# Latent product: slots of an adaptive chunk used alternately with those of a latent chunk, and two q or k products in one PSUM bank

## The chip, the cores and the metric

The kernel runs on one core of one Trainium2 chip. The metric is the device time of one execution in microseconds, and the median of the runs is what is compared. The engines are TensorE (PE; its weight loads are PEld), VectorE (DVE), ScalarE (ACT), GpSimd (POOL) and SyncE (SP), which issues most loads. One profiled execution gives the trace; its times are microseconds from the start of its span.

## What is computed

Two blocks act on 256 tokens of width 2048. The first (attention, a recurrent group, a layer of 16384 experts of which rows are gathered) isn't touched by the change. The second has two layers, each with adaptive parameters: a shift, a scale and a gate computed from a conditioning vector. Cut to what matters here:

```python
def ada_params(cond, w, b):
    mod = jax.nn.silu(cond) @ w + b          # 2048 -> 6144, for each layer
    return jnp.split(mod, 3, axis=-1)

xm_l = x_lat * (1.0 + sc_l) + sh_l
proj = xm_l @ w_in                           # 256 x 2048 @ 2048 x 7184
q, k, v, o, z_m, gates, u_p, z_p = split(proj)
qk = silu(dwconv_centered(concatenate([q, k], -1), conv_qk))   # three taps along the tokens
```

The product `xm_l @ w_in` for the latent tokens is the stage in question; the mLSTM scan and a pooling branch use its parts.

## The kernel before

**Plan.** Everything that TensorE multiplies by comes through a ring of four slots in SBUF, 128 x 2048 fp32 (1024 KB) each. The class `Plan` (lines 89 to 160) numbers in advance each load, each PSUM unit (a unit takes bank number unit modulo 8) and each "piece". `make_plan` writes the order out by hand, and the engines' programs follow the same order. SP goes through `plan.loads` in order (line 488 issues): load n waits for the release of load n-4, which was in the same place of the ring, and nothing behind it is issued before that.

**Adaptive chunks.** The 24 chunks of 512 columns of the adaptive weights take four slots each. `ada_chunk(c)` multiplies each slot with the conditioning vectors in four column groups of 32 (line 645); a slot is released as soon as TensorE has used it. Then `ada_rows` on ACT copies the result, `ada_turn(c)` on TensorE turns it (line 656), and `ada_columns` on ACT adds the bias (line 1041). Chunk 15 and chunks 16 to 21 are spread over the latent stage: `LAT_ADA` says ahead of which latent chunk each one is computed.

**Latent chunks.** `LAT` is the order: l_q 0 and 1, l_k 0 and 1, l_g, l_v 0 and 1, l_u 0 and 1, l_o 0 and 1, l_zp 0 and 1, l_z 0 and 1. A chunk is 512 columns of the weights with all 2048 rows, in four slots; each slot is two pieces. The fp32 product is made of three products of halves: ACT copies a piece to its hi half (`split_hi`, line 1016), DVE (q, k, v; line 1494) or POOL (u, o, zp, z; line 543) subtracts to get the lo half, and TensorE does `split_chunk` (line 623): for each of 16 row tiles, three matmuls for each output. The buffer of pieces holds four. A latent slot is released by the lo half of its second piece.

For q and k the outputs are features by tokens, four of 128 x 256, each in a PSUM unit of its own; for the others two of 128 x 512. DVE's `conv_unit` (lines 1802 to 1804) reads the q and k units in the next chunk's time, among the lo halves. Behind l_u 0 TensorE needs the gate rows, which come from a chain on ACT and DVE (lines 1878 to 1904, 1329); behind l_u 1, l_o 0, l_o 1 and l_zp 0 follow the mLSTM heads (lines 834, 841, 856), and behind l_zp 1 the pooling products (lines 903, 915). After l_z 0 TensorE transposes y, which DVE has to have ready (until line 2025).

ACT's part is `latent_hi`: hi halves 0 to 3, then `ada_columns`, the evacuation of the chunk before, `ada_rows`, then hi halves 4 to 7.

Of the kernel before, what the change touches and what calls it, by code (L numbers as in the profile page):

```python
# [64 lines left out]
def row_slot(n):  # L65
# [14 lines left out]
       ("l_o", 0), ("l_o", 1), ("l_zp", 0), ("l_zp", 1), ("l_z", 0), ("l_z", 1))  # L80
LAT_ADA = {("l_q", 0): 15, ("l_k", 0): 16, ("l_v", 0): 17, ("l_u", 0): 18, ("l_o", 0): 19, ("l_zp", 0): 20,
           ("l_z", 0): 21}
LAT_HEAD = {("l_u", 1): 0, ("l_o", 0): 1, ("l_o", 1): 2, ("l_zp", 0): 3}
# [21 lines left out]
class Plan:  # L105
# [26 lines left out]

    def split_chunk(self, name, c, units):

        for i in range(units):
            self.unit[name, c * units + i] = len(self.unit)
        eng = "pool" if name in LO_POOL else "dve"
        for j in range(8):
            self.piece[name, c, j] = len(self.piece)
            self.lo[eng] += 1  # L140
            self.piece_lo.append((eng, self.lo[eng]))
            if j % 2:
                self.slot[name, c, j // 2] = len(self.loads)
                self.loads.append((name, c, j // 2, 2048))
                self.release.append(("lo_" + eng, self.lo[eng]))
            if j < 7:
                self.piece_used += 1
                self.piece_release.append(("piece", self.piece_used))
            else:
                self.piece_release.append(("unit", self.unit[name, (c + 1) * units - 1]))  # L150
# [27 lines left out]
def make_plan():  # L178
# [31 lines left out]
    p.units("x2T", 8)  # L210
    for step in LAT:
        name, c = step
        if step in LAT_ADA:
            p.gemm(("ada", LAT_ADA[step]), 1, 4, 1, 2048)
        if name == "l_g":
            p.gemm("l_g", 1, 1, 1, 256)
        else:
            p.split_chunk(name, c, 4 if name in ("l_q", "l_k") else 2)
        if step in LAT_ADA:
            p.turn(LAT_ADA[step])  # L220
        if step == ("l_u", 0):
# [28 lines left out]
def build(nc, t, out):  # L250
    plan = make_plan()
    ctx = ExitStack()
    with ctx:
# [297 lines left out]
        def _(pe):  # L551
# [47 lines left out]

            def split_chunk(name, c, hi, lo, features, later=None):  # L600

                n_units = 4 if features else 2
                o = [open_unit((name, n_units * c + i)) for i in range(n_units)]
                for j in range(8):
# [6 lines left out]
                    for kk in range(2):  # L611
                        k = 2 * j + kk
                        whi, wlo = pc[:, 512 * kk:512 * kk + 512], pc[:, 1024 + 512 * kk:1536 + 512 * kk]
                        for i in range(n_units):
# [19 lines left out]

            def ada_chunk(c):


                name = ("ada", c)
                if c == 0:
                    pe.wait_ge(sem("cond_ready"), 1)  # L640
                o = open_unit((name, 0))
                for s in range(4):
                    sl = slot_of(name, 0, s)
                    for j in range(4):
                        m = nc.tensor.matmul(o[32 * j:32 * j + 32, :], cond_s[:, 2 * (4 * s + j):2 * (4 * s + j) + 32],  # L645
                                             sl[:, j * 512:(j + 1) * 512], start=(s == 0), stop=(s == 3))
                    if s < 3:
                        m.then_inc(sem("slot_used"), 1)
                close(m, (name, 0))

# [304 lines left out]
        def _(act):  # L955
# [337 lines left out]
            def latent_hi(name, c, evac=None):  # L1293

                at = LAT.index((name, c))
                before = LAT_ADA.get(LAT[at - 1]) if at else None
                if name == "l_g":
# [4 lines left out]
                else:  # L1302
                    split_hi(name, c, 0, 4)
                if before is not None:
                    ada_columns(before)
                if evac is not None:
                    evac(LAT[at - 1][1])
                if (name, c) in LAT_ADA:
                    ada_rows(LAT_ADA[name, c])
                if name != "l_g":  # L1310
# [115 lines left out]
        def _(dve):  # L1426
# [370 lines left out]

            def conv_unit(name, i, dst, c0):

                wait_unit(dve, (name, i))  # L1800
                x_, y = bank((name, i))[:, 0:S], dst[:, i, :]
# [3 lines left out]
                give(m, (name, i))  # L1805
                gave(dve, (name, i))
                dve.sem_inc(sem("conv_ready"), 1)

# [38 lines left out]
            def lo_and_conv(name, c, units):  # L1847
# [9 lines left out]
            split_lo("l_q", 0)  # L1857
            lo_and_conv("l_q", 1, [("l_q", i, QL2, 0) for i in range(4)])
            lo_and_conv("l_k", 0, [("l_q", i, QL2, 0) for i in range(4, 8)])
            lo_and_conv("l_k", 1, [("l_k", i, KL2, 8) for i in range(4)])  # L1860
# [4 lines left out]
            lo_and_conv("l_v", 0, [("l_k", i, KL2, 8) for i in range(4, 8)])  # L1865
            split_lo("l_v", 1)
# [349 lines left out]
```

## Time and profile before

| | us |
|---|---|
| median of 3 runs (lowest, highest) | 3024.66 (3022.16, 3025.05) |
| the profiled execution | 3025.71 |
| its span | 3023.9 |
| TensorE busy | 1648.0 (54%) |
| DVE busy | 1992.5 (66%) |
| POOL busy | 1244.4 (41%) |
| mean granted TensorE clock | 0.764 |

The page cuts the span into 40 slices of 75.6 us and gives the busy share of each in tenths. The timeline shows instructions in order of time, with the idle time before each and who ended it in brackets. The view of waits sums those idle times by waiter and releaser. The chain of waits goes back from the end to what released each step. The windows give busy time, number of instructions, granted clock (1.00 is 2.4 GHz), DMA share and GB/s of a stretch.

### The profile page before, as it was taken

To read this page: it belongs to the slowest core of one execution; us is meant where nothing else is said; L and a number is where in the kernel's file an instruction comes from. 1 tells how busy PE (TensorE), PEld (TensorE's weight loads), DVE (VectorE), ACT (ScalarE), POOL (GpSimd) and SP (SyncE) were. 2 spreads that over 40 slices of the span, in tenths; PEclk is the share of its full clock that TensorE was granted. 3 is DMA by queue.
4 is the path that set the end of the run, shared out by engine and by line. 5 is a ranking of instruction groups with operands and counts; after the bars stand their busy time and mean duration, and the time that the engine had idled before them with its cause. 6 is when DMAs were issued, how large, how long until landed. Compare 5 with 4: busy or idle time off the path is not lost.

```text
span 3023.9 us, 20189 instructions
## 1 busy us (share of the span) xinstructions
PE 1648.0 (54%) x7536; PEld 1219.8 (40%) x7536; DVE 1992.5 (66%) x2358; ACT 524.0 (17%) x783; POOL 1244.4 (41%) x598
## 2 busy tenths in 40 slices
PE   7994888794700440000000000048999889899987
PEld 3773443681600120000000000038777678588876
DVE  1364120388999979999999999975343536644556
ACT  1014200110100000000000000023333334345432
POOL 0000000033488768888888888820054550000000
PEclk9997789895855775555555555569999999899998
DMA  5442845399999999999999999965544555655543
GB/s 219 141 159 93 333 185 198 138 393 422 421 422 422 417 421 422 421 422 422 422 422 422 422 422 422 422 272 183 196 180 167 183 182 194 256 195 195 195 141 110
DMA packets 122753, 882.31 MB, mean 292 GB/s; under 512 B 13728, under 2 KB 14240, under 8 KB 16416
## 3 DMA queue, kind: packets, MB, share of 16 engines
q0 software_dynamic: 73728, 536.90, 42.7%
q1 hardware_dynamic: 45920, 326.91, 29.5%
q10 hardware_dynamic: 3008, 17.21, 1.5%
q8 instruction: 59, 0.97, 0.1%
q14 instruction: 38, 0.31, 0.0%
HBM read 878.88 MB, written 2.10 MB: 291 GB/s over the span
## 4 chain that ended last, share of the span: by engine, by line
PE 44%; POOL 30%; DMA 10%; DVE 8%; issue 5%; ACT 2%; DVEq 0%; SPq 0%; ACTq 0%
PE psum L623 24%; POOL W L519 18%; POOL early_rows L519 12%; PE psum L593 7%; PE psum L576 6%; DMA early_rows<-in_peer_u,W 3%; DMA ring<-in_ada 3%; DMA W<-in_peer_u,W 3%; PE psum L645 2%; PE psum L856 1%; DVE W L1789 1%; DMA W<-in_peer_v,W 1%; PE psum L696 1%; PE psum L841 1%; PE psum L656 1%
## 5 line engine op out<-in xcount | busy, mean ns | idle before, releaser
L519 POOL DMA_INDIRECT W<-in_peer_u,W x150 | 297.3, 1982 | 746.4 <-DVEq L1771 611.3
L623 PE MATMUL psum<-split,hi 128*128 128x512 f32 x1664 | 524.8, 397 | 46.5 <-POOL split L543 31.5
L696 PE MATMUL psum<-cst,X 128*128 128x128 f32 x64 | 10.4, 340 | 909.8 <-DVEq L1842 909.8
L1494 DVE TENSOR_TENSOR split<-ring,split 128x1024 fp32r<-128x1024 f32 x208 | 252.5, 1225 | 287.3 <-ACT split L1016 285.2
L696 PEld LDWEIGHTS psum<-cst,X 128*128 128x128 f32 x64 | 10.1, 183 | 910.7 <-DVEq L1842 910.7
L1838 DVE SCALAR_TENSOR_TENSOR X<-W,X 128x2048 f32<-128x2048 f32 x154 | 362.1, 2351 | 22.7 <-DMA W<-in_peer_v,W 4.1
L1016 ACT ACTIVATE split<-ring 128x1024 fp32r<-128x1024 f32 x272 | 284.1, 1057 | 490.4 <-PE psum L623 377.7
L1789 DVE CUSTOM_DVE_ANT_0 W<-W,XN 128x2048 f32<-128x2048 f32 x150 | 340.7, 2290 | 42.9 <-DMA W<-in_peer_u,W 42.1
L623 PEld LDWEIGHTS psum<-split,hi 128*128 128x128 f32 x1664 | 318.9, 192 | 118.9 <-issue 52.1
L519 POOL DMA_INDIRECT W<-in_peer_v,W x154 | 338.2, 2196 | 47.5 <-issue 47.5
L543 POOL TENSOR_TENSOR split<-ring,split 128x1024 fp32r<-128x1024 f32 x64 | 157.0, 2478 | 313.8 <-ACT split L1016 313.7
L593 PE MATMUL psum<-HT,ring 128*128 128x256 f32 x1280 | 279.5, 381 | 10.2 <-ACT HT L1196 9.0
L593 PEld LDWEIGHTS psum<-HT,ring 128*128 128x128 f32 x1280 | 244.2, 191 | 44.4 <-ACT HT L1196 9.1
L1789 DVE CUSTOM_DVE_ANT_0 early_rows<-early_rows,XN 128x2048 f32<-128x2048 f32 x106 | 241.5, 2291 | 24.2 <-DMA early_rows<-in_peer_u,W 23.0
L1838 DVE SCALAR_TENSOR_TENSOR X<-early_rows,W,X 128x2048 f32<-128x2048 f32 x102 | 239.8, 2351 | 14.8 <-DMA early_rows<-in_peer_v,W 2.1
L519 POOL DMA_INDIRECT early_rows<-in_peer_u,W x106 | 206.3, 1946 | 91.7 <-DVE W L1789 61.5
L519 POOL DMA_INDIRECT early_rows<-in_peer_v,W x102 | 222.9, 2186 | 31.7 <-issue 31.7
L623 PE MATMUL psum<-split,lo_odd 128*128 128x512 f32 x512 | 200.4, 391 | 0.0
L530 POOL TENSOR_TENSOR lo_odd<-W,hi 128x512 fp32r<-128x512 f32 x8 | 11.5, 1436 | 400.3 <-ACT hi L998 400.2
L645 PE MATMUL psum<-ring,cond_s 128*32 128x512 f32 x768 | 120.1, 748 | 84.0 <-DMA ring<-in_ada 84.0
L576 PE MATMUL psum<-ring,W 128*128 128x512 f32 x336 | 148.2, 604 | 10.3 <-DVEq L1692 7.5
L623 PE MATMUL psum<-split,lo_even 128*128 128x512 f32 x320 | 128.4, 401 | 0.0
(303 smaller groups left out, 2200.1 us busy)
## 6 DMA issues: line engine op xcount, KB each, us to landing
ring<-in_ada SPq DMA_DIRECT2D x96, 1024.0 KB, 7.5
ring<-in_odd SPq DMA_DIRECT2D x48, 1024.0 KB, 4.9
ring<-in_w_out SPq DMA_DIRECT2D x16, 1024.0 KB, 4.9
ring<-in_pq SPq DMA_DIRECT2D x16, 1024.0 KB, 7.6
ring<-in_c_k SPq DMA_DIRECT2D x16, 1024.0 KB, 8.1
ring<-in_c_v SPq DMA_DIRECT2D x16, 1024.0 KB, 7.9
ring<-in_w_even SPq DMA_DIRECT2D x16, 1024.0 KB, 4.8
ring<-in_w_odd SPq DMA_DIRECT2D x16, 1024.0 KB, 4.8
```

The lines of the kernel that those rows point to most:

```text
L519: nc.gpsimd.indirect_dma_start(row, None, t["peer_" + table], bass.IndirectOffsetOnAxis(ap=EIDX[:, c:c + 1], axis=0),).then_inc(full, 16)
L543: nc.gpsimd.tensor_tensor(split[:, to + 1024:to + 2048], ring[:, at:at + 1024], split[:, to:to + 1024], ALU.subtract).then_inc(sem("lo_poo ...
L576: m = nc.tensor.matmul(o[tt][:, 0:width], lhs[:, k, tt * P:(tt + 1) * P], sl[:, kk * width:(kk + 1) * width], start=(k == 0), stop=(k == s ...
L593: m = nc.tensor.matmul(o[m4][:, 0:S], sl[:, kk * 512 + m4 * P:kk * 512 + m4 * P + P], rhs[:, k, :], start=(k == 0), stop=(k == KD - 1))
L623: m = nc.tensor.matmul(dst, lhs, rhs, start=(k == 0 and b == 0), stop=(k == KD - 1 and b == 2))
L645: m = nc.tensor.matmul(o[32 * j:32 * j + 32, :], cond_s[:, 2 * (4 * s + j):2 * (4 * s + j) + 32], sl[:, j * 512:(j + 1) * 512], start=(s = ...
L656: m = nc.tensor.matmul(o[:, 2 * a:2 * a + 2], ADAROW[:, a * P:(a + 1) * P], const("sum4"), start=True, stop=True)
L696: m = nc.tensor.transpose(o[:, kk * S + tt * P:kk * S + (tt + 1) * P], src(2 * i + kk, tt), IDENT)
L1016: A(split[:, 2048 * (n % PIECES):2048 * (n % PIECES) + 1024], ring[:, at:at + 1024], ACT.Copy)\
L1494: TT_(split[:, to + 1024:to + 2048], ring[:, at:at + 1024], split[:, to:to + 1024], ALU.subtract)\
L1789: V.tensor_tensor_reduce(out=row, in0=row, in1=xn3[:, tt, :], scale=1.0, scalar=0.0, op0=ALU.mult, op1=ALU.add, accum_out=PACT[:, c:c + 1])\
L1838: STT(x3[:, tt, :], row, PACT[:, c:c + 1], x3[:, tt, :], ALU.mult, ALU.add)\
```

## The change

Chunk 15 (`LAT_FIRST`) is computed ahead of l_q 0 as before. Each of chunks 16 to 21 is now computed within a latent chunk: 16 in l_q 0, 17 in l_k 0, 18 in l_v 0, 19 in l_u 0, 20 in l_o 0, 21 in l_zp 0. Its four slots are loaded alternately with the latent slots (latent, adaptive, latent, ...), and TensorE uses one after every second piece. An adaptive slot is still released by TensorE. The turn of a chunk comes after the next latent chunk (`LAT_ADAS`). The four q or k outputs of a chunk go to two PSUM units, two halves of 256 columns in each; only the first matmul into a bank carries the start flag, and the unit is closed by its second half. DVE reads both halves and gives the bank back once.

```diff
-LAT_ADA = {("l_q", 0): 15, ("l_k", 0): 16, ("l_v", 0): 17, ("l_u", 0): 18, ("l_o", 0): 19, ("l_zp", 0): 20,
-           ("l_z", 0): 21}
+LAT_FIRST = 15
+LAT_ADA = {("l_q", 0): 16, ("l_k", 0): 17, ("l_v", 0): 18, ("l_u", 0): 19, ("l_o", 0): 20, ("l_zp", 0): 21}
+LAT_ADAS = (LAT_FIRST,) + tuple(LAT_ADA.get(step) for step in LAT)
...
+    def ada_slot(self, c, s):
+
+        name = ("ada", c)
+        if s == 0:
+            self.unit[name, 0] = len(self.unit)
+        self.slot[name, 0, s] = len(self.loads)
+        self.loads.append((name, 0, s, 2048))
+        if s < 3:
+            self.used += 1
+            self.release.append(("used", self.used))
+        else:
+            self.release.append(("unit", self.unit[name, 0]))
+
+    def split_chunk(self, name, c, units, ada=None):
...
                 self.release.append(("lo_" + eng, self.lo[eng]))
+                if ada is not None:
+                    self.ada_slot(ada, j // 2)
...
-    for step in LAT:
+    p.gemm(("ada", LAT_FIRST), 1, 4, 1, 2048)
+    for at, step in enumerate(LAT):
         name, c = step
-        if step in LAT_ADA:
-            p.gemm(("ada", LAT_ADA[step]), 1, 4, 1, 2048)
...
-            p.split_chunk(name, c, 4 if name in ("l_q", "l_k") else 2)
-        if step in LAT_ADA:
-            p.turn(LAT_ADA[step])
+            p.split_chunk(name, c, 2, LAT_ADA.get(step))
+        if LAT_ADAS[at] is not None:
+            p.turn(LAT_ADAS[at])
...
-                                dst = o[i][:, 0:S]
+                                dst = o[i // 2][:, S * (i % 2):S * (i % 2) + S]
...
-                                m = nc.tensor.matmul(dst, lhs, rhs, start=(k == 0 and b == 0),
-                                                     stop=(k == KD - 1 and b == 2))
-                            if k == KD - 1:
-                                close(m, (name, n_units * c + i))
+                                m = nc.tensor.matmul(dst, lhs, rhs,
+                                                     start=(k == 0 and b == 0 and not (features and i % 2)),
+                                                     stop=(k == KD - 1 and b == 2 and not (features and i % 2 == 0)))
+                            if k == KD - 1 and not (features and i % 2 == 0):
+                                close(m, (name, 2 * c + (i // 2 if features else i)))
                     if j < 7:
                         m.then_inc(sem("piece_used"), 1)
+                    if ada is not None and j % 2:
+                        ada_slot(ada, j // 2)
...
+            def ada_slot(c, s):
+
+                name = ("ada", c)
+                if c == 0 and s == 0:
+                    pe.wait_ge(sem("cond_ready"), 1)
+                o = open_unit((name, 0)) if s == 0 else bank((name, 0))
+                sl = slot_of(name, 0, s)
+                for j in range(4):
+                    m = nc.tensor.matmul(o[32 * j:32 * j + 32, :], cond_s[:, 2 * (4 * s + j):2 * (4 * s + j) + 32],
+                                         sl[:, j * 512:(j + 1) * 512], start=(s == 0), stop=(s == 3))
+                if s < 3:
+                    m.then_inc(sem("slot_used"), 1)
+                else:
+                    close(m, (name, 0))
...
-            ada_chunk(LAT_ADA[LAT[0]])
+            ada_chunk(LAT_FIRST)
             wait_split("x2T")
 
             def latent_chunk(name, c):
 
-                ada = LAT_ADA.get((name, c))
-                if ada is not None and (name, c) != LAT[0]:
-                    ada_chunk(ada)
                 if name == "l_g":
                     split_gates("l_g", LO_EVEN)
                 else:
-                    split_chunk(name, c, HI, LO_EVEN, name in ("l_q", "l_k"))
-                if ada is not None:
-                    ada_turn(ada)
+                    split_chunk(name, c, HI, LO_EVEN, name in ("l_q", "l_k"), ada=LAT_ADA.get((name, c)))
+                before = LAT_ADAS[LAT.index((name, c))]
+                if before is not None:
+                    ada_turn(before)
...
+            def conv_unit(name, i, dst, c0, per=1):
+
+                key, half = (name, i // per), i % per
+                if half == 0:
+                    wait_unit(dve, key)
+                x_, y = bank(key)[:, S * half:S * half + S], dst[:, i, :]
...
+                if half == per - 1:
+                    give(m, key)
+                    gave(dve, key)
+                    dve.sem_inc(sem("conv_ready"), per)
+                else:
+                    seq(m)
```

## Rows read from the trace of the kernel before

**Rows 1.** The page, slices: busy tenths of TensorE in 40 slices.
```profile
PE   7994888794700440000000000048999889899987
```

**Rows 2.** Waits of TensorE, 2040 to 2470 us: total, times, longest.
```profile
PE psum L623 <- POOL split L543: 31.5, 5, 7.3
PE psum L623 <- DVE W L1804: 9.7, 3, 8.8
PE psum L623 <- DVE split L1494: 3.8, 2, 3.4
PE psum L645 <- DMA ring<-in_ada: 2.1, 1, 2.1
...
PE psum L880 <- ACT W L1329: 0.5, 1, 0.5
```

**Rows 3.** Timeline: first matmul of l_zp 1; one lo half on DVE.
```profile
2399.48 0.77 PE L623 MATMUL psum<-split,hi 128*128 128x512 f32 x1 [7.30 <-POOL split L543]
...
2042.78 1.23 DVE L1494 TENSOR_TENSOR split<-ring,split 128x1024 fp32r<-128x1024 f32 x1 [1.72 <-ACT split L1016]
```

**Rows 4.** The chain ahead of l_o 0: start us, us, what.
```profile
2273.69 1.04 PE psum L645 x8
...
2274.75 4.94 DMA ring<-in_l_o
...
2279.71 1.06 ACT split L1016
...
2280.84 2.36 POOL split L543
```

**Rows 5.** Windows: busy (instructions) of PE, PEld, DVE, ACT, POOL, granted clock, DMA share, GB/s.
```profile
2151.60:2158.00 6.40, 6.36 (x16) 5.04 (x17) 5.85 (x9) 3.29 (x4) 0.00 (x0) 0.54 1.01 426
2158.00:2177.00 19.00, 19.00 (x90) 15.84 (x88) 8.78 (x12) 13.69 (x15) 0.00 (x0) 1.00 0.51 172
...
2199.60:2203.10 3.50, 3.50 (x33) 0.88 (x32) 0.00 (x0) 0.00 (x0) 0.00 (x0) 1.00 0.37 103
```

**Rows 6.** Windows of line 623: l_q 1, l_k 0, three undisturbed chunks, five late ones.
```profile
2045.00:2070.00 25.00, 23.27 (x192) 23.10 (x192) 1.00 0.38 129
2081.00:2107.50 26.50, 25.23 (x192) 25.06 (x192) 0.91 0.48 172
...
sum 66.30, PE 65.78 PEld 53.55; mean PE 21.93 PEld 17.85
...
sum 122.00, PE 119.49 PEld 96.74; mean PE 23.90 PEld 19.35
```

**Rows 7.** Timeline: four loads issued together, and TensorE using the first and second.
```profile
2594.46 2.90 SPq L488 DMA_DIRECT2D ring<-in_ada  x4
...
2599.34 1.07 PE L645 MATMUL psum<-ring,cond_s 128*32 128x512 f32 x8 [2.37 <-DMA ring<-in_ada]
2601.72 1.94 PE L645 MATMUL psum<-ring,cond_s 128*32 128x512 f32 x8 [1.32 <-DMA ring<-in_ada]
```

**Rows 8.** The chain that ends with the gate rows on TensorE.
```profile
2209.05 1.04 ACT split L1016
...
2214.92 2.72 DVE W L1888
...
2228.66 0.69 DVE W L1899
...
2233.90 0.41 PE psum L880 x4
```

**Rows 9.** Timeline: single rows of POOL, ACT, TensorE and DVE.
```profile
2206.78 21.31 POOL L543 TENSOR_TENSOR split<-ring,split 128x1024 fp32r<-128x1024 f32 x8 [192.54 <-ACT split L1016]
...
2237.54 0.67 ACT L1041 ACTIVATE ada<-psum,col 128x2 f32<-128x2 f32 x4
...
2434.71 3.64 PE L645 MATMUL psum<-ring,cond_s 128*32 128x512 f32 x32
...
2438.73 0.69 DVE L2025 TENSOR_TENSOR XN<-XN,W 128x512 f32<-128x512 f32 x1
```

More of the change, by code:

```diff
@@ L130, in gemm @@
                     self.release.append(("unit", self.unit[name, (c + 1) * units - 1]))
-    def split_chunk(self, name, c, units):
+    def ada_slot(self, c, s):
[10 more added lines that the diff above has]
+    def split_chunk(self, name, c, units, ada=None):
         for i in range(units):
@@ L598, in feature_gemm, with split_chunk @@
                             m.then_inc(sem("slot_used"), 1)
-            def split_chunk(name, c, hi, lo, features, later=None):
-                n_units = 4 if features else 2
-                o = [open_unit((name, n_units * c + i)) for i in range(n_units)]
+            def split_chunk(name, c, hi, lo, features, later=None, ada=None):
+                o = [open_unit((name, 2 * c + i)) for i in range(2)]
                 for j in range(8):
@@ L613, in split_chunk @@
                         whi, wlo = pc[:, 512 * kk:512 * kk + 512], pc[:, 1024 + 512 * kk:1536 + 512 * kk]
-                        for i in range(n_units):
+                        for i in range(4 if features else 2):
                             a = slice(i * P, i * P + P)
@@ L633, in split_gemm @@
                     split_chunk(name, c, HI, lo, False)
+            def ada_slot(c, s):
[11 more added lines that the diff above has]
+                    close(m, (name, 0))
             def ada_chunk(c):
[L638 to L641, printed above, removed]
                 for s in range(4):
[L643 to L649, printed above, removed]
+                    ada_slot(c, s)
             def ada_turn(c):
@@ L1295, in latent_hi @@
                 at = LAT.index((name, c))
-                before = LAT_ADA.get(LAT[at - 1]) if at else None
+                turned = LAT_ADAS[at - 1] if at else None
                 if name == "l_g":
@@ L1303, in latent_hi @@
                     split_hi(name, c, 0, 4)
-                if before is not None:
-                    ada_columns(before)
+                if turned is not None:
+                    ada_columns(turned)
                 if evac is not None:
                     evac(LAT[at - 1][1])
-                if (name, c) in LAT_ADA:
-                    ada_rows(LAT_ADA[name, c])
+                if LAT_ADAS[at] is not None:
+                    ada_rows(LAT_ADAS[at])
                 if name != "l_g":
@@ L1796, in dots_done @@
                 dve.sem_inc(sem("dots_ready"), 1)
-            def conv_unit(name, i, dst, c0):
-                wait_unit(dve, (name, i))
-                x_, y = bank((name, i))[:, 0:S], dst[:, i, :]
+            def conv_unit(name, i, dst, c0, per=1):
[3 more added lines that the diff above has]
+                x_, y = bank(key)[:, S * half:S * half + S], dst[:, i, :]
                 seq(TS(y, x_, column("conv_qk", 16 + c0 + i), None, ALU.mult))
@@ L1804, in conv_unit @@
                 m = STT(y[:, 0:S - 1], x_[:, 1:S], column("conv_qk", 32 + c0 + i), y[:, 0:S - 1], ALU.mult, ALU.add)
-                give(m, (name, i))
-                gave(dve, (name, i))
-                dve.sem_inc(sem("conv_ready"), 1)
+                if half == per - 1:
[4 more added lines that the diff above has]
+                    seq(m)
             topk(0, 0)
@@ L1857, in _ @@
             split_lo("l_q", 0)
-            lo_and_conv("l_q", 1, [("l_q", i, QL2, 0) for i in range(4)])
-            lo_and_conv("l_k", 0, [("l_q", i, QL2, 0) for i in range(4, 8)])
-            lo_and_conv("l_k", 1, [("l_k", i, KL2, 8) for i in range(4)])
+            lo_and_conv("l_q", 1, [("l_q", i, QL2, 0, 2) for i in range(4)])
+            lo_and_conv("l_k", 0, [("l_q", i, QL2, 0, 2) for i in range(4, 8)])
+            lo_and_conv("l_k", 1, [("l_k", i, KL2, 8, 2) for i in range(4)])
             slot = plan.slot["l_g", 0, 0]
@@ L1864, in _ @@
                 GATE_W[:, 0:256], ALU.subtract).then_inc(sem("gate_w_lo"), 1)
-            lo_and_conv("l_v", 0, [("l_k", i, KL2, 8) for i in range(4, 8)])
+            lo_and_conv("l_v", 0, [("l_k", i, KL2, 8, 2) for i in range(4, 8)])
             split_lo("l_v", 1)
```

## The prediction

> **What bounds the kernel now.** I read the page's slices first, to find what each stage waits for [rows 1]. From slice 8 to slice 26 TensorE has next to nothing to do: that is the stage of gathered rows, which the diff doesn't touch. The latent products begin at 2018.7 us, in slice 27, and from there TensorE is busy at eight to nine tenths. What is left to win there is its idle time, and the time it spends at the lower clock. The view of waits of TensorE over the latent stage (2040 to 2470 us) has nearly all of its idle time [rows 2]: 31.5 us in five waits on POOL's lo halves, 9.7 in three on a convolution of DVE (one of them 8.8), 3.8 in two on DVE's lo halves (one of them 3.4), 2.1 for an adaptive slot, and 0.5 for the gate rows. Of the five on POOL the longest, 7.30 us, stands ahead of l_zp 1, which has no adaptive chunk ahead of it [rows 3]. The other four (31.5 - 7.3 = 24.2) stand ahead of l_u 0, l_o 0, l_zp 0 and l_z 0; the 8.8 ahead of l_k 0, the 3.4 ahead of l_v 0, and the 2.1 inside the adaptive chunk ahead of l_v 0. All of these belong to an adaptive chunk: 24.2 + 8.8 + 3.4 + 2.1 = 38.5 us.
>
> The releaser named (a lo half) is the last link only. The chain [rows 4] has the whole of it for l_o 0: TensorE uses an adaptive slot (1.04), only then can SP load a latent slot into that place of the ring of four (4.94), then come ACT's hi half (1.06) and POOL's lo half (2.36). All four places held the adaptive chunk, so nothing of the latent chunk was there early.
>
> Each pause costs a second time. Right behind one the granted clock is 0.54, which is the 1.2 GHz level for nearly the whole stretch, and from 2158 us it is 1.00 [rows 5]. By the windows of line 623 [rows 6] an undisturbed chunk takes 23.27 us (l_q 1) or 21.93 (mean of l_v 1, l_u 1, l_o 1). Behind a pause l_k 0 takes 25.23, and l_v 0, l_u 0, l_o 0, l_zp 0 and l_z 0 take 119.49 together, where 5 x 21.93 is 109.65. That is 1.96 + 9.84 = 11.8 us.
>
> **The change part by part.** The adaptive products 16 to 21 move from ahead of their latent chunk into the latent chunk before, one slot after every two pieces. LAT_FIRST (15) stays. 24 slots are used in a new place; the number of matmuls, loads and turns is the same.
>
> *The pauses.* Loads now alternate, latent and adaptive. Load n waits for the release of load n-4, so the first two latent slots of a chunk wait for lo halves of pieces 1 and 5 of the plain chunk before it, both long before that chunk ends. The tight one is the fourth. SP issues in order, so it goes one issue behind the third adaptive load, which waits until TensorE has used adaptive slot 0; call that moment e. Four loads issued together at 2594.46 landed at 2599.34 and 2601.72, 4.88 and 7.26 us later [rows 7]. So the latent slot is there at e + 7.26. With 1.06 of ACT, 2.36 of POOL [rows 4] and 0.2 for handing on, piece 6 is ready at e + 10.9; with DVE's 1.23 [rows 3], e + 9.8. TensorE reaches piece 6 after four pieces (4 x 21.93/8 = 10.97) and two adaptive slots (2 x 1.04): e + 13.05. The slack is 2.1 us on POOL's chunks and over 3 on DVE's. The third latent slot waits for an early lo half and has more; an adaptive slot issued at e is wanted a whole period after it lands. l_v 0 stands behind the one slot of l_g: its second adaptive load is asked for when l_g ends and its third latent load right behind, wanted 13.05 us later, so the slack is the same. I put all 38.5 us at gone, and with them the 11.8 of low clock.
>
> *Two products in one bank.* l_q 1 and l_k 1 wait for a convolution (9.7 - 8.8 = 0.9 us [rows 2]) that must empty the bank they open. Half as many banks are opened, and the one taken then was emptied a chunk earlier: 0.9 gone. Matmuls of 256 columns write half a bank in the trace as well, so the sharing itself costs nothing; DVE's convolutions stay 24 x 3 instructions.
>
> *Two waits with chains of their own.* l_v 1 waits 3.8 - 3.4 = 0.4 us for ACT, which has gates and table loads between piece 7 of l_v 0 and piece 0 of l_v 1. Three adaptive slots (3.1 us) now lie in that time, so it goes. Behind l_u 0 TensorE waits 0.5 us: its gate rows come from a chain that starts with ACT's last early hi half at 2209.05 and ends on TensorE at 2233.90 [rows 8], 24.85 us. Now ada_columns stands ahead in it (0.67 [rows 9]): 25.5 us from the end of l_v 1. TensorE gets there after a chunk and four slots, 21.93 + 4.16 = 26.1, and the turn between. This wait goes too, with 0.6 us and a turn to spare; it is what is late next. Together 0.9 us.
>
> In that chain a DVE scan took 2.72 us while POOL ran (2206.78 to 2228.09) and 0.69 once it had stopped [rows 8, 9]. POOL will be less dense there, so the chain can only shorten. But l_z 0 no longer waits behind an adaptive chunk, and its eight subtractions on POOL fall on the DVE chain that ends at 2439.42 and is wanted at 2434.7 + 21.9 = 2456.6 [rows 9]. If each holds DVE up for its whole 2.36 us, it ends at 2458.3: a bound of 2 us, taken at nothing. The Trainium skill, SBUF — State Buffer, section "Who interferes with whom", says that a DVE instruction with two SBUF inputs is locked out for the whole of a GpSimd instruction that reads SBUF. The trace agrees, as the scans show.
>
> *Cost of the slots.* A whole adaptive chunk takes TensorE 3.64 us [rows 9], a single slot in the chain 1.04 [rows 4]. Before, six chunks: 6 x 3.64 = 21.8. Now 24 x 1.04 = 25.0, 3.1 us more. From below: the next matmul starts while the last of the slot are in flight, as inside a chunk, 3.64/4 a slot: no more than before. From above: the array is emptied on both sides of each slot. I bound that by one more overhang on each side, of the size by which a single slot exceeds a quarter chunk, 1.04 - 0.91 = 0.13, and to be safe by twice that: 24 x 0.26 = 6.2 on top, 9.3 in all. I take 3.1, since that is what a single slot measured. The Trainium skill, TensorEngine Tiling (Array Packing), section "Key Properties", says that changing the tiling mode drains TensorE. It speaks for the upper end, and by it the sum would come out 6.2 us later.
>
> *Untouched.* The 7.3 us ahead of l_zp 1 stay with their low clock: ACT stands there behind DMA issues and two evacuations, not behind the ring. So do the pauses behind l_z 1.
>
> **The sum.** 38.5 + 11.8 + 0.9 + 0.9 = 52.1, less 3.1 = 49.0 us. The profiled execution took 3025.7 us (3023.9 of span and 1.8 around it), which gives 2976.7. It lies 1.0 above the median of the runs shown, less than can be told apart, so the number stands for that too.
>
> **The rivals.**
> (1) Both sides of each slot drain the array: 3025.7 - 52.1 + 9.3 = 2982.9. For it, the rule above; against it, the single slot at 1.04.
> (2) The ring becomes the wait inside the chunks. The tight slot has 2.1 us. With ACT held by an evacuation, or a slower landing, piece 6 is late in four to six chunks by 2 to 3 us, each with about 2 of low clock: 16 to 30 us given back, 2993 to 3007. Against it: loads back to back land every 2.38 us [rows 7], so the eight of a mixed chunk need 19 of its 26 us.
> (3) Slower. The slots, with their few columns of weights, let the granted clock fall inside the chunk. A chunk at 1.2 GHz costs another 21.9 us, so from 49/21.9 = 2.2, say three chunks, the gain is gone; all six give 2976.7 + 131 = 3108. Against it: the clock stayed at 1.00 through a whole adaptive chunk [rows 5].
> (4) The change doesn't do what it says: with SP's queue in order the latent slots are asked for no earlier, and the pauses only move inside the chunks. The 0.9 of the banks goes, the rest stays: 3025. Against it: a latent slot's release is now a lo half of the chunk before.
>
> **How the numbers follow.** Forecast within its bounds (2973 to 2981) 0.76; rival 1 0.08; rival 2 0.09; rival 3 0.03; rival 4 0.04. The predicted time is 2976.7. The range of 8 in 10 goes from 2970 (no cost of slots, and the few us by which whole runs differ) to 2990, which takes in rival 1 and what is milder than rival 2. About 0.2% (6 us) is what a measurement of this kernel can tell from no change. Faster by more: forecast and rivals 1 and 2, 0.93; within it 0.04 (rival 4); slower 0.03 (rival 3).
>
> **What would show it.** Right: no idle stretch over 1 us on TensorE between 2045 us and the end of l_zp 0, at a granted clock of 1.00; a mixed chunk spans 21.93 + 4 x 1.04 = 26.1 us (27.4 for l_k 0) from its first to its last matmul. Rival 1 shows as mixed chunks of 27.3 us without idle time; rival 2 as pauses on line 623 ahead of piece 6, released by POOL or DVE; rival 3 as a clock of 0.5 in a chunk that has no pause; rival 4 as pauses of the old sum inside the chunks. The prediction is wrong if a pause stays ahead of any of the six chunks, or if a new one over 2 us appears before the gate rows or the transposes of yT.

## The result, and the profile after

| | before | after |
|---|---|---|
| median (lowest, highest), us | 3024.86 (3022.16, 3027.40) | 2978.30 (2971.41, 2981.27) |
| the profiled execution, its span | 3025.71, 3023.9 | 2981.27, 2979.5 |
| TensorE, DVE, POOL busy | 1648.0, 1992.5, 1244.4 | 1640.4, 2007.3, 1247.6 |
| mean granted TensorE clock | 0.764 | 0.768 |

The ratio of the times is 0.9843, with a 95% interval of 0.9824 to 0.9862: faster by 46.6 us, where 48.0 (3024.7 - 2976.7) was forecast. Between the two profiled executions it is 44.4 us. The changed kernel run a second time gave 2977.86 (2972.93 to 2983.31), ratio 0.9851 (0.9835 to 0.9867).

Below, "the stage" is the time from the first matmul of l_q 0 to the first matmul of the product that follows l_z 1 (line 637 with w_even). It went from 484.82 us (2018.74 to 2503.56) to 436.54 (2019.90 to 2456.44), 48.28 less. Both profiled executions of the changed kernel have the same 436.54. What lies outside it differs by several us from execution to execution: over all the kernels below the stage began between 2014.7 and 2020.0 us. So the stage tells apart what the medians can't, and each experiment is read by both. Every other kernel has one profiled execution only: a difference of 1 us or less between two stages is a single reading.

Page, slices after, busy tenths of TensorE and its granted clock. Slices are 74.5 us now. Against [rows 1] the latent stage (from the 28th digit) has seven digits of 9 where there were 8s among them. The clock shows 9 in all seven, as it did before: tenths of a whole slice are too coarse for what the clock gave back, and the windows below have it.

```profile
PE   7995879794800260000000000009999999899987
...
PEclk9997789895855685555555555559999999899998
```

Waits of TensorE from 2040 to 2470 us, the same view and stretch as [rows 2] (total, times, longest). Lines have moved: 623 is 637, 645 is 660, 543 is 558, 1494 is 1512, 1016 is 1034.

```profile
PE psum L637 <- POOL split L558: 7.1, 1, 7.1
PE psum L637 <- DVE split L1512: 3.6, 2, 2.0
PE psum L716 <- DVEq L2056: 2.4, 1, 2.4
PE psum L933 <- issue: 0.8, 1, 0.8
```

31.5 us in five waits on POOL have become 7.1 in one. It is the one ahead of l_zp 1. The waits for a convolution, an adaptive slot and the gate rows are gone. Of the 3.6 on DVE, 2.0 stand ahead of w_even, which lay beyond this stretch before; the other 1.6 is a wait that grew, ahead of l_v 1.

The chain through l_u 0 (start us, us, what). Ahead of such a chunk [rows 4] had load, hi and lo half in a row. Now it is TensorE alone: two pieces, an adaptive slot, two pieces. The last row is l_u 1, undisturbed.

```profile
2188.32 5.61 PE psum L637 x24
2193.92 1.00 PE psum L660 x8
2194.92 5.66 PE psum L637 x24
...
2220.35 21.80 PE psum L637 x96
```

Windows of the line 637 (us, PE and PEld busy, granted clock, DMA share, GB/s) for mixed l_k 0, undisturbed l_k 1, mixed l_u 0, undisturbed l_u 1, and l_zp 1. The first four answer to [rows 5, 6]: the clock is 1.00 in all of them. Of the chunks from l_k 0 on only l_zp 1, behind its pause, has less, 0.90.

```profile
2074.62:2102.28 27.66, 23.95 (x193) 23.14 (x193) 1.00 0.61 229
2102.28:2125.50 23.22, 23.22 (x192) 23.01 (x192) 1.00 0.55 187
...
2188.30:2214.90 26.60, 22.82 (x96) 17.56 (x96) 1.00 0.67 252
2220.30:2242.15 21.85, 21.85 (x96) 17.72 (x95) 1.00 0.46 168
...
2364.40:2388.79 24.39, 24.25 (x96) 19.57 (x96) 0.90 0.51 173
```

Where the 48.3 us went is told by one window over the stage of each kernel (us, PE busy, clock):

```profile
2019.90:2456.44 436.54, 422.64 (x2404) 0.99 0.57 207
```

The same window of before:

```profile
2018.74:2503.56 484.82, 432.49 (x2404) 0.93 0.51 186
```

Idle time fell from 52.33 (484.82 - 432.49) to 13.90, by 38.4. The same 2404 instructions are busy for 9.9 less.

### The profile page after: what moved, and what is told of

It reads as the page before. It is cut to its first block, busy times and chain, and to the rows that moved or that the text cites. A ratio compares the mean times of both kernels' runs of the same rounds, so it can differ in the third digit from the quotient of the medians.

```text
span 2979.5 us, 20177 instructions
## 1 busy us (share of the span) xinstructions
PE 1640.4 (55%) x7536; PEld 1204.4 (40%) x7536; DVE 2007.3 (67%) x2358; ACT 523.0 (18%) x783; POOL 1247.6 (42%) x598
## 4 chain that ended last, share of the span: by engine, by line
PE 45%; POOL 30%; DMA 10%; DVE 7%; issue 5%; ACT 2%; SPq 0%; DVEq 0%; ACTq 0%
PE psum L637 25%; POOL W L534 18%; POOL early_rows L534 12%; PE psum L608 7%; PE psum L591 7%; DMA early_rows<-in_peer_u,W 3%; DMA ring<-in_ada 3%; DMA W<-in_peer_u,W 3%; PE psum L660 2%; PE psum L874 1%; DVE W L1807 1%; PE psum L716 1%; DMA W<-in_peer_v,W 1%; PE psum L676 1%; PE psum L859 0%
## 5 line engine op out<-in xcount | busy, mean ns | idle before, releaser
L1861 DVE SCALAR_TENSOR_TENSOR X<-W,X 128x2048 f32<-128x2048 f32 x154 | 362.1, 2351 | 22.7 <-DMA W<-in_peer_v,W 3.8
L1807 DVE CUSTOM_DVE_ANT_0 early_rows<-early_rows,XN 128x2048 f32<-128x2048 f32 x106 | 241.5, 2291 | 23.9 <-DMA early_rows<-in_peer_u,W 22.7
L694 PE MATMUL psum<-HT,ring 128*8 128x256 f32 x64 | 15.9, 415 | 202.2 <-DVE W L1824 202.2
```

The source lines that it names most:

```text
L1807: V.tensor_tensor_reduce(out=row, in0=row, in1=xn3[:, tt, :], scale=1.0, scalar=0.0, op0=ALU.mult, op1=ALU.add, accum_out=PACT[:, c:c + 1])\
L1861: STT(x3[:, tt, :], row, PACT[:, c:c + 1], x3[:, tt, :], ALU.mult, ALU.add)\
```

## The experiments

### Each part alone

The changed kernel again, for what two samples of one kernel differ by:

> The changed kernel once more, beside the three others on one chip, to have their differences against it. Its four runs so far spread over 10 us (2971.4 to 2981.3) where before spreads over 5. Theory: 2978, with a spread of several us that comes from where the low clock of the start of the latent stage ends, not from the ring. Rival: the ring's tight slots land late in some runs, so that the trace shows pauses in mixed chunks that the first one doesn't have.

Told above: stage 436.54 both times, medians 0.4 us apart. No pause stands in a mixed chunk of either, so the rival falls. The theory on the spread isn't borne out either: the start of the stage is the same, and the two profiled executions are only 1.1 us apart. Where the 10 us between single executions come from isn't shown.

Two products in one bank alone, with the adaptive chunks ahead of their latent chunk as before:

```diff
-                o = [open_unit((name, n_units * c + i)) for i in range(n_units)]
+                o = [open_unit((name, 2 * c + i)) for i in range(2)]
...
-                                dst = o[i][:, 0:S]
+                                dst = o[i // 2][:, S * (i % 2):S * (i % 2) + S]
...
```

> Only the pairing of q and k products in one bank, in the kernel before; the adaptive chunks stay ahead of their latent chunks. My prediction priced this part at 0.9 us (the two waits of 0.44). Read again, the trace of before says more: ahead of l_k 0 the lo half of piece 0 was done some 4 us before the convolution that freed the bank, so the pause of 8.8 us should shrink to 4.5 or so. Theory: 3024.9 - 0.9 - 4.2 = 3020. Rival (the price in the prediction): 3024, with the 8.8 us still there, ended by a load.

Measured: 3017.38 us (3012.41 to 3022.13) beside 3023.46, ratio 0.9979 (0.9970 to 0.9987); stage 478.23, 6.6 less. The forecast gave this part 0.9. Its two waits of 0.44 are gone as said. What the forecast missed stands in the chain ahead of l_k 0. Before:

```profile
2070.88 6.41 DMA ring<-in_c_k
...
2078.40 1.23 DVE split L1494
2079.63 0.41 DVE W L1802
...
2080.06 0.49 DVE W L1803
...
2080.57 0.49 DVE W L1804
...
2081.32 3.75 PE psum L623 x16
```

With the banks alone:

```profile
2069.34 4.88 DMA ring<-in_c_k
...
2075.33 1.24 DVE split L1494
...
2076.70 8.36 PE psum L622 x47
```

The 8.8 us ahead of l_k 0 ended with a convolution (1802 to 1804) that had to empty the bank. DVE does it behind the lo half of a later load, the one that waited for the second adaptive slot, and its own 1.4 us come on top. With the bank free TensorE starts on the first lo half, and the pause is 4.84. Three waits make up 5.3 of the 6.6: this pause (3.9), the two of 0.44 (0.9) and the one for the gate rows, which is gone here too (0.5). The forecast had put all 8.8 to the adaptive chunk. With both parts that is the same sum, but the two share this pause.

The alternate slots alone, four banks for q and k as before:

```diff
-            p.split_chunk(name, c, 2, LAT_ADA.get(step))
+            p.split_chunk(name, c, 4 if name in ("l_q", "l_k") else 2, LAT_ADA.get(step))
...
```

> Only the alternate slots, with four banks for a q or k chunk as before. Theory: the pauses of the ring go as in the changed kernel, but TensorE now reaches l_q 1, l_k 0 and l_k 1 without delay and has to wait for convolutions of the chunk before: about 2.3 us ahead of l_q 1 (two convolutions), 0.5 ahead of l_k 0 and of l_k 1, with a little low clock: 2978.3 + 4 = 2982. Rival: the parts simply add up, 2978.3 + 0.9 = 2979. A third one, that the pairing carried most of the gain, would give over 3000.

Measured: 2986.02 us (2984.88 to 2990.95), ratio 0.9885 (0.9870 to 0.9899); stage 443.54, 41.3 less. Waits of TensorE, 2040 to 2470 us:

```profile
...
PE psum L638 <- DVE W L1824: 5.0, 3, 2.7
PE psum L638 <- DVE split L1512: 3.2, 2, 2.0
...
```

Without the pairing the convolution waits don't merely stay at 0.9 us: ahead of l_q 1 it is 2.65 and ahead of l_k 1 1.95, because the last pieces of the mixed chunk come late and DVE's convolutions stand behind their lo halves. The parts add up (6.6 + 41.3 = 47.9 of 48.3), but the pairing is worth 7.0 (443.54 - 436.54) beside the slots, not 0.9. That they add up is partly chance. The slots alone take the whole pause ahead of l_k 0 but for 0.44, so the 3.9 that the banks alone take from it count in both parts. In their place the pairing takes away the waits ahead of l_q 1 and l_k 1 that grew with the slots (3.7 more), and the low clock behind the first of them: l_q 1 takes 25.6 us there and 23.3 in the changed kernel.

### What a slot costs

Slots used in twos, behind pieces 3 and 7 (loads: latent, latent, adaptive, adaptive). The same 24 slots, half the places where the shape of the matmuls changes:

```diff
-                    if ada is not None and j % 2:
+                    if ada is not None and j % 4 == 3:
+                        ada_slot(ada, j // 2 - 1)
                         ada_slot(ada, j // 2)
...
```

> The changed kernel with its slots in twos: loads go latent, latent, adaptive, adaptive, and TensorE uses two adaptive slots after piece 3 and two after piece 7, so the array changes over 24 times instead of 48. In the trace of the changed kernel a slot stretches the chunk by 1.0 us in its own row and by about 0.2 in the matmuls around it. Theory (the 0.2 and the tail belong to the change-over): about 0.3 us less for each of 12 slots, 4 us, and the last latent slot of l_v 0 lands early, so that ACT's gate rows are no longer late for l_v 1, another 1.6: 2978.3 - 5.6 = 2973. Rival (cost is per slot): 2977. Rival (a second adaptive slot holds the ring too long): pauses ahead of piece 4 of the mixed chunks and over 2985.

Measured: 2970.56 us (2969.83 to 2973.53), ratio 0.9832 (0.9819 to 0.9845); stage 430.27, which is 6.3 below the changed kernel. Chain through l_u 0 (the view's edge cuts the first row, which shows 44 of 48):

```profile
2179.97 9.99 PE psum L638 x44
2189.97 1.85 PE psum L662 x16
2191.82 11.11 PE psum L638 x48
2202.93 1.85 PE psum L662 x16
```

Two slots take 1.85 instead of 2.00, and four pieces 11.11 instead of 2 x 5.66. l_u 0 takes 25.86 where it took 26.58 (2188.32 to 2214.90), 0.7 less; over the six mixed chunks it is 4.7, which puts the 24 slots at 22.7 us (27.4 - 4.7, below), next to the 21.8 of six whole chunks. l_q 0, whose start is at the low clock in both kernels, has 1.1 of the 4.7, some of it because that clock ended sooner; the other five chunks are 3.5 shorter. The wait ahead of l_v 1 is gone as well (1.6) and l_zp 1 is 0.6 shorter; 0.39 appears ahead of the transposes of yT. By the medians the step is 7.3 us, by the ratios 0.9832 to 0.9851, whose intervals overlap. So the stage shows this gain and the whole time doesn't quite.

### The wait ahead of l_v 1

In the chain after, TensorE stands 1.59 us ahead of l_v 1 where it stood 0.41:

```profile
2142.92 1.04 PE psum L660 x8
...
2144.35 8.13 DMA ring<-in_c_v
...
2152.50 2.01 ACT split L1034 x2
...
2161.23 1.73 ACT W L1292
...
2163.05 1.05 ACT split L1034
...
2164.12 1.24 DVE split L1512
...
2165.49 22.04 PE psum L637 x96
```

This is the tight latent slot of l_v 0: issued when TensorE had used the first adaptive slot (e, 2143.96), landed at e + 8.5 and not e + 7.26. ACT then makes the last two hi halves of the chunk, the gates (lines 1220 to 1286) and the silu of the k convolutions (line 1292), with their table loads, and only then piece 0 of l_v 1. That is 13.0 us from landing (2152.48) to matmul, and TensorE was ready at 2163.90. If so, the gates put elsewhere must take the wait away.

```diff
-            latent_hi("l_v", 0)
-            gate_rows_l(0)
+            latent_hi("l_v", 0, gate_rows_l)
```

(the gates between hi halves 3 and 4 of l_v 0)

> The changed kernel with ACT's evacuation of the gates (two evacuations, three activations, two table loads) moved from behind piece 7 of l_v 0 to between its pieces 3 and 4, where ACT was idle. The changed kernel waits 1.59 us ahead of l_v 1. Theory: hi halves 6 and 7 of l_v 0 now come late because their slot lands at the tight end of the ring, and ACT's gate work, queued behind them, makes l_v 1 late; moved, the wait goes: 1.6 us less, 2976.5. Rival (the wait is DVE's or the load's own): it stays, 2978.

Measured: 2975.59 us (2971.40 to 2979.38) beside 3023.76, ratio 0.9838 (0.9825 to 0.9852); stage 435.49, 1.05 less. Waits of TensorE, 2040 to 2470 us:

```profile
...
PE psum L637 <- DVE split L1511: 0.9, 1, 0.9
...
PE psum L716 <- DVEq L2048: 0.8, 1, 0.8
```

The wait of 1.59 is gone (the 0.9 is ahead of w_even), so it was ACT's order behind a late load, as the theory said. 0.77 of it comes back as a wait ahead of the transposes of yT. By the time alone the step can't be told from none.

### The pause ahead of l_zp 1, and what is late next

The forecast left it, since ACT stands there behind DMA issues and evacuations. Four hi halves of l_zp 1 put ahead of them:

```diff
             dec_exps(3)
+            split_hi("l_zp", 1, 0, 4)
             wait_unit(act, ("ms", 7))
             act.dma_start(w(4096, 2048), t["pool_w"]).then_inc(sem("poolw_loaded"), 16)
...
-            latent_hi("l_zp", 1)
+            latent_hi("l_zp", 1, first=False)
...
```

> The changed kernel with hi halves 0 to 3 of l_zp 1 ahead of ACT's wait for the last mLSTM products, its DMA issues and the evacuation of l_zp 0. The 7.1 us ahead of l_zp 1 and the 2.3 of low clock behind them were said to belong to ACT's order, not to the ring. Theory: both go, 9.5 us less, 2968.5. Rival: DVE's normalisation ahead of the transposes of yT, which ended only 2.5 us ahead of TensorE in the changed kernel, becomes the bound and gives back most of it: 2975.

Measured: 2973.64 us (2968.70 to 2977.27), ratio 0.9826 (0.9813 to 0.9840); stage 435.71, 0.8 less. The pause shrank from 7.12 to 2.88, and the low clock behind it went. What is left looks like a bank that an evacuation holds: ACT's first evacuation of l_zp 0 (0.6 us, behind a table load of 1.3) ended 0.1 us ahead of the matmul. The view names no releaser, so that is read from the times alone. But 3.03 us appeared ahead of the transposes of yT. The chain of DVE that makes y starts only after the heads, and TensorE now comes sooner. So the rival of the expectation came out.

All three together (slots in twos, gates, hi halves):

> Slots in twos (2970.6 measured), with both changes of ACT's order. Theory: the order ahead of l_zp 1 brings its 9.5 us here as well, and the gates' order nothing, since the twos had already taken the wait ahead of l_v 1: 2961. Rival: in the kernel with twos DVE's normalisation was late by 0.4 us already, so the gain ends in a wait ahead of the transposes of yT: 2967 or more.

Measured: 2975.32 us (2972.45 to 2976.65), ratio 0.9835 (0.9822 to 0.9848); stage 433.83, worse than the twos alone (430.27), where 2961 or, by the rival, 2967 and more was expected. The wait ahead of yT is 6.10: its chain also waits for the weights mh_g, a load that took 9.7 us here where it took 3.4 in the changed kernel, behind pool_w and two loads of the ring.

The twos with only two early hi halves, behind the issue of pool_w:

```diff
             act.dma_start(w(4096, 2048), t["pool_w"]).then_inc(sem("poolw_loaded"), 16)
+            split_hi("l_zp", 1, 0, 2)
...
-            latent_hi("l_zp", 1)
+            latent_hi("l_zp", 1, first=2)
...
```

> Slots in twos, with only hi halves 0 and 1 of l_zp 1 put forward, and behind ACT's load of the pooling weights, not ahead of it. In the version with four hi halves put forward, the load of the norm's gains stood in the queues behind the pooling weights and two ring loads and took 9.7 us in place of 3.4, and DVE's normalisation began that much later. Theory (the load's place in the queues was the fault): it takes 6 us or less now, TensorE starts l_zp 1 about 4 us earlier at full clock, 6 us in all, and some 4 to 5 of them end in a wait ahead of the transposes of yT: 2969, with a stretch from the first latent matmul to the first of w_even of 429 us, against 430.3 and 433.8. Rival (the putting forward itself is at fault, by POOL's earlier subtractions): as slow as with four, 433 and 2974.

Measured: 2975.18 us (2972.67 to 2975.36) beside 3020.97, ratio 0.9843 (0.9830 to 0.9857); stage 435.77. Timeline (start, us, what, idle before and who ended it), TensorE ahead of l_zp 1 and of yT, and the start of the chain on DVE:

```profile
2351.87 0.70 PE L638 MATMUL psum<-split,hi 128*128 128x512 f32 x2 [2.88 <-issue]
...
2415.41 3.67 PE L718 MATMUL psum<-cst,XN 128*128 128x128 f32 x16 [5.72 <-DVEq L2052]
...
2354.29 2.74 DVE L2029 TENSOR_TENSOR XN<-XN,W 128x1024 f32<-128x1024 f32 x1 [4.00 <-DMA W<-in_mh_g]
```

Against the twos alone 4.3 us of wait are won (7.15 to 2.88) and 5.3 lost (0.39 to 5.72), and the transposes and l_z 1 behind the new wait run 2.8 longer at the lower clock. That is 3.8 of the 5.5 us by which the stage is longer; the rest lies in l_q 0 (0.5) and behind l_z 1 (1.2). The load of mh_g was there 5.3 us after its issue (2349.03 to 2354.29), as the theory wanted, and the stage is as long as the rival had it all the same. So the load's place wasn't the fault. What is late is the DVE chain itself. Two rows of it in the changed kernel, the same instruction beside POOL's subtractions and without:

```profile
2378.17 2.32 DVE L1456 TENSOR_SCALAR stat<-stat 128x4 f32<-128x4 f32 x1
...
2394.19 0.17 DVE L1456 TENSOR_SCALAR stat<-stat 128x4 f32<-128x4 f32 x1
```

There are two such runs of 13 small instructions (four columns each). Where POOL subtracts without a break they are stretched one after the other, each from 0.2 to 2.3: four in the first run, from 2373.47 to 2382.84, and four more in the second. So the remedy tested is fewer of them: one inverse square root on eight columns for both halves of y in place of two on four.

```diff
-                seq(V.tensor_reduce(st(205, 4), heads(junk), AX.X, ALU.add))
-                rstd(st(205, 4), st(205, 4), MD, LN_EPS)
-                seq(TT_(heads(y), heads(y), all_of(st(205, 4), MD), ALU.mult))
+                seq(V.tensor_reduce(st(205 + 4 * tt, 4), heads(junk), AX.X, ALU.add))
+            rstd(st(205, 8), st(205, 8), MD, LN_EPS)
+            for tt in range(TT):
+                y = HM[:, tt, :]
+                seq(TT_(heads(y), heads(y), all_of(st(205 + 4 * tt, 4), MD), ALU.mult))
```

With the twos alone:

> Slots in twos, with DVE's normalisation of both token tiles ahead of the transposes of yT computing its reciprocal root once, on eight columns, and not twice on four (13 DVE instructions fewer, of which a few met a POOL subtraction and took 2.3 us each). Theory (POOL stretches that chain, and it stands just at the edge): the chain ends 4 to 10 us earlier, the 0.4 us ahead of the transposes goes and nothing else changes: 2970. Rival (the chain waits for TensorE's pooling products anyway): it ends no earlier.

Measured: 2975.42 us (2972.07 to 2976.41), ratio 0.9842 (0.9828 to 0.9855); stage 430.76, against 430.27 without it. The chain ends some 16 us before TensorE is there, and nothing is won, since only 0.39 us was waited for. A control: the edit is worth nothing by itself.

With the twos and the two early hi halves:

> Both of the former together: two hi halves of l_zp 1 put forward, and one reciprocal root. Theory (what was won ahead of l_zp 1 was lost to DVE's normalisation): the wait ahead of the transposes of yT goes and the whole 6 us stay: a stretch of 424 us and 2964. Rival: the wait there has another releaser and stays: 429 and 2969.

Measured: 2967.17 us (2962.43 to 2967.99) beside 3020.97, ratio 0.9812 (0.9798 to 0.9825); stage 425.87, 9.9 less than with the two early hi halves and the old chain (435.77). Its interval lies wholly below that kernel's (0.9830 to 0.9857). The theory's 424 and 2964 are missed by 2 and 3 us. Waits of TensorE, 2040 to 2470 us, and after them, from the timeline, DVE's instruction of above, now on eight columns:

```profile
PE psum L638 <- issue: 2.9, 1, 2.9
PE psum L718 <- DVEq L2061: 2.4, 1, 2.4
PE psum L638 <- DVE split L1515: 2.0, 1, 2.0
...
```

```profile
2378.17 0.17 DVE L1459 TENSOR_SCALAR stat<-stat 128x8 f32<-128x8 f32 x1
```

No wait is left ahead of yT. This kernel has the shortest stage of all here, 10.7 us less than the changed kernel, and by the ratios (0.9812 beside 0.9843) it is 9 us faster. Against the twos alone only the stage tells it apart (425.87 and 430.27); the intervals of the ratios overlap. Of the kernels tried, the pause ahead of l_zp 1 was worth something only together with the shorter DVE chain.

### Is the low clock the pause's doing?

The forecast priced 11.8 us of low clock as following from the pauses. A rival: it comes from the adaptive chunk and would have stayed. In the kernel before, matmuls that nobody reads fill the pauses; they write the bank that the chunk's own first matmul then overwrites, so what is computed stays the same.

```diff
-                o = [open_unit((name, n_units * c + i)) for i in range(n_units)]
+                o = [open_unit((name, n_units * c))]
+                for _ in range(FILL.get((name, c), 0)):
+                    nc.tensor.matmul(o[0], hi[:, 0, 0:P], hi[:, 0:2, :], start=True, stop=True)
+                o += [open_unit((name, n_units * c + i)) for i in range(1, n_units)]
...
```

(24 of them ahead of l_k 0, l_u 0, l_o 0, l_zp 0 and l_z 0, 12 ahead of l_v 0)

> The kernel before, with 24 matmuls of 512 columns on data that is there already (12 ahead of l_v 0), into the bank that the chunk then overwrites, in each of the six pauses. Loads, pauses and everything else stay; TensorE is only kept at work in them, some 5.4 us in pauses of 6 to 9. Theory (the low clock comes from the pause, 11.8 us in six chunks): the granted clock stays at 1.00 in them, 11.8 us less, of which about 1.2 ends in the wait for the gate rows: 3013. Rival (the low clock belongs to the loads or to the chunk itself): 3024 and the same chunk times.

Measured: 3019.24 us (3013.29 to 3025.93), ratio 0.9987 (0.9977 to 0.9996); stage 478.40, 6.4 less though nothing was started earlier. Windows of the line of the chunks, l_k 0, then l_o 0, l_zp 0 and l_z 0:

```profile
2077.80:2102.60 24.80, 24.76 (x192) 0.93 0.50 178
...
2279.30:2301.36 22.06, 22.04 (x96) 1.00 0.70 248
2355.15:2377.21 22.06, 22.02 (x96) 1.00 0.78 296
2437.20:2459.27 22.07, 22.02 (x96) 1.00 0.67 241
```

Behind filled pauses the chunks take 22.0 us at a clock of 1.00, although the adaptive chunk still stands ahead of them. So the pause takes the clock down and the adaptive chunk does not. l_k 0 shows the other side: there 3.08 us stayed unfilled, the clock fell to 0.93 in the mean and the chunk took 24.8. The six late chunks together take 134.8 where they took 144.7 (25.23 + 119.49, [rows 6]), 9.9 of the 11.8. Not all reached the end, and the time missed the 3013 expected: the wait for the gate rows grew from 0.47 to 2.09, because TensorE comes to them sooner while their chain stays. The other 1.9 of what the stage lacks (9.9 - 1.6 - 6.4) is in small waits and wasn't followed up.

## Why the prediction was right, point by point

The time came within 1.6 us of the forecast and well inside the range, and the mechanism was right: the pauses went, and the low clock with them. But two terms of the sum were too good by 4.0 us together (the slots and the wait ahead of l_v 1), and low clock that the sum had left out gave 3.6 back. That part of the nearness is luck. By my own signs the forecast didn't hold in full: one idle stretch over 1 us stood in the stage, the 1.59 ahead of l_v 1.

One reading in it is wrong and carries nothing: TensorE isn't empty from slice 8 on. The digits 9, 4 and 7 stand there, and the empty stretch runs from the 16th digit to the 26th [rows 1].

The stage, term by term:

| term | forecast | measured |
|---|---|---|
| pauses of the adaptive chunks | 38.5 | 38.4 |
| low clock behind them | 11.8 | 12.5 |
| bank waits | 0.9 | 0.9 |
| ahead of l_v 1 | 0.4 | -1.2 |
| gate rows | 0.5 | 0.5 |
| slots | -3.1 | -5.5 |
| not named: other idle time; other matmuls | 0 | -0.2; 2.9 |
| sum | 49.0 | 48.3 |

**The pauses.** Waits of seven places (8.78, 2.06, 3.43, 6.09, 6.07, 5.97, 6.04) are all zero after: 38.4. No wait stands within a mixed chunk, so rival 2 (the ring) and rival 4 fall. Its slack was thinner than I had worked out, though: the tight load landed 8.5 us after e in l_v 0 and 8.7 in l_u 0, not 7.26. In l_u 0 POOL had piece 6 ready at 2207.20 and TensorE wanted it at 2208.24, 1.0 us later and not 2.1.

**The clock.** Before, the six late chunks had 144.72; an undisturbed one of after takes 23.22 or 21.81, and 144.72 - 23.22 - 5 x 21.81 is 12.5. The clock is 1.00 in the mixed chunks from l_k 0 on, so rival 3 falls: slots with 32 columns of weights don't take it down. Low clock had also lain on work that the sum left out: the heads (line 841, now 859) went from 16.6 to 14.9 us, the transposes of line 696 from 5.0 to 3.9, those of line 866 from 4.3 to 3.7. Those are 3.4 together. The table's 2.9 is what is left of the busy time once the other terms are taken out, and small losses elsewhere, such as 0.4 in l_zp 1, go off it.

**The slots: mis-sized.** A mixed chunk takes 26.5 us (l_u 0 26.6) and not 26.1, l_k 0 27.66 and not 27.4. l_q 0 is 4.24 longer than in the kernel before, and the others are 4.44, 4.64, 4.77, 4.64 and 4.64 longer than an undisturbed chunk (23.22 or 21.81): 27.4 in all, where six whole adaptive chunks took 21.8. So the step costs 5.5 and not 3.1. The single slot has its 1.00, next to the 1.04 that I took, but the two pieces behind it take 5.66 instead of 5.45. That lies between my value and the upper end (9.3). The Trainium skill's rule in TensorEngine Tiling (Array Packing), "Key Properties", that changing the tiling mode drains TensorE, is borne out in kind: with half as many changes of shape the extra over whole chunks falls from 5.5 us to 0.9, or from 4.9 to 1.4 without l_q 0, where the clock plays in. That it is a drain and nothing else at the change isn't shown. Rival 1, the same mechanism, had too high a price: it asked for chunks of 27.3 us.

**Ahead of l_v 1: the step failed.** I wrote that three adaptive slots "now lie in that time, so it goes". They give TensorE more time, but they also put ACT behind a load that comes later. The wait grew by 1.2, and moving the gates removed it.

**The banks: right in the sum, wrong alone.** With the slots, the l_k 0 pause went as a whole whoever got the credit. Alone the pairing is worth 6.6, and beside the slots 7.0. The row of 8.8 us in [rows 2] names line 1804 as its releaser; I took that wait for the ring's and didn't ask which of its links belong to the convolution.

**What is late next.** I named the gate rows with 0.6 us and a turn to spare; they did arrive in time. For the chain ahead of yT I gave "a bound of 2 us, taken at nothing". It ended at 2420.5 and TensorE wanted it at 2423.0: nothing was paid, by 2.5 us. Every further gain upstream then met it (0.39, 0.77, 3.03, 5.72, 6.10).

## What to carry to other kernels

When a consumer frees a shared ring only at the end of a side job, spread the side job's slots among the main ones; the gain is the idle time plus the low clock behind it, so price a pause at what the chunk behind it takes over an undisturbed one. Ask of every pause which links of its chain each part of a change takes away, since two parts may share one pause and neither row tells their worth alone. After a gain, write down the slack of the next two chains: here shortening the next pause by itself made the stage longer (435.8 us against 430.3), and with the chain behind it shortened too it gave the shortest stage (425.9).

## What the runs showed of the hardware, unexpected

A change of shape costs the neighbours. Two pieces between single slots took 5.66 us and four behind double ones 11.11, where 5.45 and 10.90 are undisturbed: 0.2 us per interruption, on top of 1.00 for one slot and 1.85 for two.

The same pause doesn't always bring the low clock. Ahead of l_zp 1 TensorE stood 2.88 us in four kernels. Windows of two us behind it (us, PE busy, granted clock, DMA share, GB/s): with all three edits the clock stayed at 1.00 and the chunk took 22.0 us,

```profile
2354.95:2356.95 2.00, 2.00 (x11) 1.00 1.03 420
```

and in the fastest kernel it fell to the 1.2 GHz level, and the chunk took 23.65:

```profile
2353.91:2355.91 2.00, 2.00 (x7) 0.76 0.94 356
2355.91:2357.91 2.00, 2.00 (x6) 0.50 0.36 143
```

Two kernels kept it and two lost it: the two that kept it had put four hi halves forward, the two that lost it two. TensorE was busy for all of the 5 us looked at shortly before the pause in each of the four. Why is open; no run was made for it.

A load issued 0.4 us behind another landed 6.8 to 9.0 us after its issue within the mixed chunks, where the four of [rows 7] gave 4.88 and 7.26. A small DVE instruction (128x4) takes 0.2 us, and 2.3 where it meets a POOL subtraction of 2.4 us; two runs of 13 of them lay in the chain that was the next bound of the stage.
